# Three places instead of four for the gathered down rows, one query tile loaded ahead, and the first block's outputs joined

## The chip, the cores and the metric

The kernel runs on one core of one Trainium2 chip. Its time is the device time of one launch, in microseconds (us), as the median of three runs. The profile is of one more execution, taken by the hardware profiler.

## The reference, cut to what matters

256 tokens of 2048 channels go through a first block (retention, mLSTM, a mixture of experts called PEER) and a second block. All of it is float32. The change touches the outputs of the retention heads and the PEER layer:

```python
def step(s, inp):                       # retention, each of 8 heads
    att = jnp.einsum('bhcd,bhsd->bhcs', qc, kc) * intra
    y = jnp.einsum('bhcs,bhse->bhce', att, vc) + jnp.einsum('bhcd,bhde->bhce', qc * q_dec, s)
...
def block(tb):                          # PEER, each block of 128 tokens
    qh = (tb @ w_query).reshape(P_BLOCK, P_HEADS, 2, P_DQ // 2)
    s = jnp.einsum('thpd,hpkd->thpk', qh, sub_keys).astype(jnp.float32)
    sv, si = lax.top_k(s, P_TOPK)
    ...                                 # 16 of 16*16 pairs for each of 8 heads: eid [128, 8, 16]
    g = jax.nn.softmax(best_s, axis=-1)
    act = jax.nn.gelu(jnp.einsum('thkd,td->thk', expert_down[eid], tb).astype(jnp.float32), approximate=False)
    return jnp.einsum('thk,thkd->td', (g * act).astype(tb.dtype), expert_up[eid])
```

For each token 8 x 16 = 128 experts are picked, and for each pick one row of `expert_down` and one of `expert_up` is needed, 2048 numbers each.

## The kernel before, in words

The program is a row of phases on one core; each engine has its own instruction stream, written out in order, and waits on semaphores. The phases are an opening (to about 450 us), the first block (450 to 909 us), the PEER layer (909 to about 2265 us) and the second block (to the end).

**First block.** TensorE runs a dense projection: each "slot" m is 24 matmuls of 128x512 (L996, L997, L998). Small groups of other work are put between slots, by tables of slot numbers (L884 to L900): `TURN_AT`, `HEAD_AT`, `Y_AT` and so on. `scores(h)` (L1036) makes a pair's attention scores, `ret_out(h)` (L1048, L1050) the output of head h in PSUM bank V + h % 2, and ScalarE copies that output out in the same slot. `turn_y(f)` transposes the finished y in fills of four 128x128 pieces; ScalarE (`copy_hi`) and VectorE (`copy_lo`) split each fill into a high and a low part. ScalarE (L722) and GpSimd (L729) also make the high and low parts of the dense weights.

**PEER.** The query projection reads `peer_query` in tiles of 128x4x512, four tiles (slots 0 to 3) for each of four chunks of 512 columns. Chunk 0 is in the weight ring. The four tiles of chunk 1 are "early" tiles in other places that are free: `query_tile` (1,0), `key_scores` (1,1), `mem_kv` (1,2), `free_query_tile` (1,3). SyncE (L1707 to L1717) issues (1,3) at once, waits for `h2_ready`, issues the other three, and then loads chunks 2 and 3 into the ring, each when its slot is given free.

Tokens lie on the partitions, two blocks of 128, so 256 picks p, in 128 groups G of two. A row transfer (`indirect_dma_start`, GpSimd) fetches the row of pick p for 128 tokens at once: 128x2048 float32, 1.05 MB. D(p) is the down row, U(p) the up row. GpSimd's order in group G is D(2G), D(2G+1), U(2G), U(2G+1) (L1747 to L1775), each with its wait ahead of it:
- D(p) (L1758) has 4 places, `down_rows`, and waits for dot p-4, which frees the place. `down_rows` lies in the 32 KB per partition that the first block used for split weights.
- U(p) (L1766) has 4 places, `up_rows`, and waits for the adding of pick p-4: even picks are added by VectorE, odd ones by TensorE.

VectorE's order in group G is dot 2G, dot 2G+1 (L2272, each waits for its landing), a piece of the list work for later heads (L1575 to L1583, L2155 to L2207), and the adding of up row 2(G-1) (L2216 the first of a block, L2219). Between a dot and the adding stand ScalarE's gelu and share (L2047, L2053, L2059) and the diagonal (L2062) by which TensorE adds the odd row (L1909).

## Time and profile before

| | |
|---|---|
| median of 3 runs | 3403.07 us (3401.09 to 3404.42) |
| profiled execution | 3401.59 us, of it 3399.8 us span |
| TensorE busy, VectorE, GpSimd | 85%, 54%, 69% of the span |
| mean granted TensorE clock | 0.919 |
| row transfers (GpSimd's queue) | 536.90 MB, 37.5% of the 16 engines' span |

The busy shares are means over phases with different limits. What bounds a phase is read from the idle time of its engines and from what ended it: a row of the profile ends with the idle time in front of a group of instructions and its releaser. In the table of windows each engine has its busy time (and its count of instructions), then come the granted clock, the busy share of the 16 DMA engines (it can read slightly over 1), and GB/s.

### The profile page before, as it was taken

Reading aid. Unit: us, or ns where it says so; the run is one execution under the profiler, and the core shown is the slowest. Engines: PE = TensorE matmul, PEld = TensorE weight load, DVE = VectorE, ACT = ScalarE, POOL = GpSimd, SP = SyncE. Lnnn points to the kernel's source line nnn. Section 1 sums busy time; section 2 is a strip of 40 time slices with the busy share of each in tenths; the row PEclk is TensorE's granted clock in tenths of the full one; section 3 lists DMA queues with packets and bytes.
Section 4 is the critical chain, followed back from the end, with each engine's and each line's share of the span. In section 5 each row is a group of like instructions: output and inputs, shape, how many; then the busy total and the mean of one; then the engine's idle time right before and its main releaser. Section 6 shows DMA issues by size and latency. Waiting matters only on the chain. (4 is left out here: it accounts for less than half of the span.)

```text
span 3399.8 us, 30787 instructions
## 1 busy us (share of the span) xinstructions
PE 2904.0 (85%) x11248; PEld 2041.8 (60%) x11248; DVE 1824.3 (54%) x2377; ACT 1145.8 (34%) x1860; POOL 2338.9 (69%) x1120
## 2 busy tenths in 40 slices
PE   6999999999986666655656776589999999999998
PEld 2787888888753333322222322248888888888887
DVE  3577537412678777778988887751147412111122
ACT  3322456544421111111221112134455444444443
POOL 0244677588667575657776677868767698888887
PEclk8999999999988888877678887889999999999999
DMA  9999855365699999999999999985545456656554
GB/s 397 338 349 335 302 173 169 126 231 192 241 420 426 425 427 425 427 427 427 412 427 427 427 427 426 427 324 188 172 154 189 138 197 194 227 190 206 190 191 164
DMA packets 308075, 1015.86 MB, mean 299 GB/s; under 512 B 21932, under 2 KB 26640, under 8 KB 241104
## 3 DMA queue, kind: packets, MB, share of 16 engines
q1 hardware_dynamic: 231336, 475.62, 40.5%
q0 software_dynamic: 73728, 536.90, 37.5%
q8 instruction: 89, 1.46, 0.2%
q10 hardware_dynamic: 2860, 1.38, 0.1%
q14 instruction: 62, 0.51, 0.0%
HBM read 1009.59 MB, written 4.24 MB: 298 GB/s over the span
## 5 line engine op out<-in xcount | busy, mean ns | idle before, releaser
L729 POOL TENSOR_TENSOR block_weights_lo<-weight_ring,block_weights_hi 128x1024 fp32r<-128x1024 f32 x596 | 1444.3, 2432 | 577.7 <-ACT block_weights_hi L722 563.1
L1909 PE MATMUL banks<-up_rows,pick_diagonal 128*128 128x512 f32 x1024 | 681.3, 827 | 438.9 <-DMA up_rows<-peer_up,picked_experts 377.5
L722 ACT ACTIVATE block_weights_hi<-weight_ring 128x1024 fp32r<-128x1024 f32 x608 | 640.8, 1059 | 997.6 <-PE banks L3063 315.9
L1909 PEld LDWEIGHTS banks<-up_rows,pick_diagonal 128*128 128x128 f32 x1024 | 262.4, 269 | 826.4 <-issue 732.5
L1766 POOL DMA_INDIRECT up_rows<-peer_up,picked_experts x256 | 483.3, 1888 | 338.6 <-DVE expert_sum L2219 113.7
L2272 DVE CUSTOM_DVE_ANT_0 down_rows<-down_rows,h_tokens 128x2048 f32<-128x2048 f32 x256 | 583.7, 2291 | 184.1 <-DMA down_rows<-peer_down,picked_experts 179.4
L1758 POOL DMA_INDIRECT down_rows<-peer_down,picked_experts x256 | 405.4, 1584 | 101.3 <-issue 78.3
L2219 DVE SCALAR_TENSOR_TENSOR expert_sum<-up_rows,pick_share,expert_sum 128x2048 f32<-128x2048 f32 x125 | 293.9, 2352 | 51.4 <-ACT pick_share L2053 45.5
L2047 ACT ACTIVATE pick_gelu<-pick_dots 128x2 f32<-128x2 f32 x127 | 25.8, 203 | 834.0 <-DVE pick_dots L2272 833.7
L2497 PE MATMUL banks<-block_weights_hi,h_T_hi 128*128 128x512 f32 x688 | 272.8, 397 | 2.3 <-POOL block_weights_lo L729 2.3
L2499 PE MATMUL banks<-block_weights_hi,h_T_lo 128*128 128x512 f32 x688 | 268.3, 390 | 0.0
L2498 PE MATMUL banks<-block_weights_lo,h_T_hi 128*128 128x512 f32 x688 | 267.9, 389 | 0.0
L3061 PE MATMUL banks<-block_weights_hi,h_T_hi 128*128 128x512 f32 x640 | 250.2, 391 | 0.0
L3063 PE MATMUL banks<-block_weights_hi,h_T_lo 128*128 128x512 f32 x640 | 249.3, 390 | 0.0
L3062 PE MATMUL banks<-block_weights_lo,h_T_hi 128*128 128x512 f32 x640 | 249.1, 389 | 0.0
L602 DVE SCALAR_TENSOR_TENSOR banks<-cond_ring,cond_T,banks 128x512 f32<-128x512 f32 x224 | 169.3, 756 | 62.4 <-DMA cond_ring<-w_ada 55.4
L996 PE MATMUL banks<-block_weights_hi,h_T_hi 128*128 128x512 f32 x504 | 200.5, 398 | 1.9 <-PEq L218 1.0
L997 PE MATMUL banks<-block_weights_lo,h_T_hi 128*128 128x512 f32 x504 | 196.7, 390 | 0.0
L3127 DVE TENSOR_TENSOR gate<-banks,p_cols 128x512 f32<-128x512 f32 x32 | 20.6, 687 | 262.4 <-PE banks L3063 262.4
L998 PE MATMUL banks<-block_weights_hi,h_T_lo 128*128 128x512 f32 x384 | 149.7, 390 | 0.0
L2497 PEld LDWEIGHTS banks<-block_weights_hi,h_T_hi 128*128 128x128 f32 x688 | 129.3, 188 | 30.4 <-POOL block_weights_lo L729 4.5
L2499 PEld LDWEIGHTS banks<-block_weights_hi,h_T_lo 128*128 128x128 f32 x688 | 129.1, 188 | 27.4
(549 smaller groups left out, 4344.5 us busy)
## 6 DMA issues: line engine op xcount, KB each, us to landing
weight_ring<-w_in SPq DMA_DIRECT2D x232, 1024.0 KB, 4.9
cond_ring<-w_ada SPq DMA_DIRECT2D x128, 512.0 KB, 6.3
weight_ring<-w_ada SPq DMA_DIRECT2D x32, 1024.0 KB, 8.6
weight_ring<-w_out SPq DMA_DIRECT2D x32, 1024.0 KB, 4.9
weight_ring<-peer_query SPq DMA_DIRECT2D x12, 1024.0 KB, 17.1
weight_ring<-w_ret_out SPq DMA_DIRECT2D x8, 1024.0 KB, 4.9
weight_ring<-w_mlstm_out SPq DMA_DIRECT2D x8, 1024.0 KB, 4.9
weight_ring<-w_mem_kv SPq DMA_DIRECT2D x8, 1024.0 KB, 11.9
```

The costliest lines, as they stand in the source:

```text
L722: act.activation(self.hi[:, self.place(slot, h)], ring.tile[:, slot, h * self.HALF:(h + 1) * self.HALF], ACT.Copy).then_inc(self.hi_ready, 1)
L729: pool.tensor_tensor(self.lo[:, at], ring.tile[:, slot, h * self.HALF:(h + 1) * self.HALF], self.hi[:, at], ALU.subtract).then_inc(ring.us ...
L1758: pool.indirect_dma_start(down[:, p % ROWS], None, io["peer_down"][0], bass.IndirectOffsetOnAxis(ap=expert[:, p:p + 1], axis=0)).then_inc( ...
L1766: pool.indirect_dma_start(up[:, p % ROWS], None, io["peer_up"][0], bass.IndirectOffsetOnAxis(ap=expert[:, p:p + 1], axis=0)).then_inc(up_l ...
L1909: mm = pe.matmul(ps[:, 4 + b], diag[:, G % 2], up[:, p % ROWS, b * CG:(b + 1) * CG], start=(G % PER_TB == 0), stop=(G % PER_TB == PER_TB - ...
L2219: dve.scalar_tensor_tensor(acc[:], up[:, p % ROWS], share[:, p:p + 1], acc[:], ALU.mult, ALU.add).then_inc(even_added, 1)
L2272: dve.tensor_tensor_reduce(down[:, p % ROWS], down[:, p % ROWS], h2[:, G // PER_TB], 1.0, 0.0, ALU.mult, ALU.add, dots[:, p:p + 1]).then_i ...
L2497: pe.matmul(out, hi, w_hi, start=(k == 0), stop=False, skip_group_check=True)
L2498: pe.matmul(out, hi, w_lo, start=False, stop=False, skip_group_check=True)
L2499: mm = pe.matmul(out, lo, w_hi, start=False, stop=(k == KB - 1), skip_group_check=True)
L3061: pe.matmul(out, hi, w_hi, start=begin, stop=False, skip_group_check=True)
L3063: mm = pe.matmul(out, lo, w_hi, start=False, stop=end, skip_group_check=True)
```

## The change

Four edits.

1. Down rows have three places instead of four, so D(p) waits for dot p-3. The three landing semaphores and their counts follow.
2. The fourth place, 8 KB per partition, becomes `tiles_ahead`, which holds query tile (2,0). It is issued by SyncE right behind the early tiles; the ring loads only three tiles of chunk 2.
3. Each early tile waits for what frees its own place: (1,3) for nothing, (1,1) until the first block's products are done (`e.split.free`), (1,0) for the second `x1_ready`, (1,2) for `h2_ready`. The order is (1,3), (1,1), (1,0), (1,2), (2,0).
4. In the first block the output of an even head is made one slot later, together with that of its odd partner (`OUT_AT`), and the eight y fills come as four in every second slot instead of two in each (`y_fill_at`).

```diff
@@ -884,6 +884,7 @@
         HEAD_AT = [STATE_AT + 3 + h for h in range(R_HEADS)]
+        OUT_AT = [HEAD_AT[h // 2 * 2 + 1] + 1 for h in range(R_HEADS)]
         LF_AT, SUM_AT = HEAD_AT[2], HEAD_AT[-1] + 1
@@ -892,6 +893,7 @@
         Y_AT = M_GATED + 1
+        y_fill_at = lambda f: Y_AT + f // 4 * 2
         columns_at = lambda g: SLOTS * (g + 1) + (3 if g == 0 else 0)
@@ -1136,7 +1138,7 @@
                 for h in range(R_HEADS):
-                    if m == HEAD_AT[h] + 1:
+                    if m == OUT_AT[h]:
                         ret_out(h)
@@ -1157,7 +1159,7 @@
                 for f in range(FILLS):
-                    if m == Y_AT + f // 2:
+                    if m == y_fill_at(f):
                         turn_y(f)
@@ -1232,7 +1234,7 @@
                 for h in range(R_HEADS):
-                    if m == HEAD_AT[h] + 1:
+                    if m == OUT_AT[h]:
                         act.wait_ge(y_done, h + 1)
@@ -1269,7 +1271,7 @@
                 for f in range(FILLS):
-                    if m == Y_AT + f // 2:
+                    if m == y_fill_at(f):
                         copy_hi(f, y_turned, lambda k: y_hi[:, k], y_hi_out)
@@ -1527,7 +1529,7 @@
                 for f in range(FILLS):
-                    if m == Y_AT + f // 2:
+                    if m == y_fill_at(f):
                         copy_lo(f, y_hi_out, lambda k: y_hi[:, k], lambda k: y_lo[:, k], y_lo_out)
@@ -1597,7 +1599,7 @@
         base, N, NB = ring.turn, HP * PEER_K // CG, CG // P
-        GROUPS, ROWS = TB * PICKS // 2, 4
+        GROUPS, ROWS, DOWN_ROWS = TB * PICKS // 2, 4, 3
         next_turn = base + N + 2 * MEM_W // CG
@@ -1620,7 +1622,7 @@
             return 8 * r - 6 if r < PEER_H else 8 * PEER_H - 6 + 6 * (r - PEER_H)
-        down, up = nc.alloc_sbuf_tensor_at("down_rows", [P, ROWS, D], F32, offset=e.split2_at), sb("up_rows", [P, ROWS, D])
+        down, up = nc.alloc_sbuf_tensor_at("down_rows", [P, DOWN_ROWS, D], F32, offset=e.split2_at), sb("up_rows", [P, ROWS, D])
         scores, acc = sb("key_scores", [P, HP, TB, PEER_K]), sb("expert_sum", [P, D])
@@ -1646,8 +1648,12 @@
                                     free_tile[:])
+        SPARE_ROWS = ROWS - DOWN_ROWS
+        ahead = nc.alloc_sbuf_tensor_at("tiles_ahead", [P, SPARE_ROWS, TILE_K, CG], F32, offset=e.split2_at + DOWN_ROWS * D * 4)
+        early_tile = {(EARLY_CHUNK, s): tile for s, tile in enumerate(early_query)}
+        early_tile.update({(EARLY_CHUNK + 1, s): ahead[:, s] for s in range(SPARE_ROWS)})
         gt2_row, GATE_ROW = spare_tile[0:1].rearrange("p a n -> p (a n)"), PER_TB - 8
-        query_tile = lambda n, s: early_query[s] if n == EARLY_CHUNK and s < len(early_query) else ring.tile[:, s]
+        query_tile = lambda n, s: early_tile[n, s] if (n, s) in early_tile else ring.tile[:, s]
 
@@ -1666,13 +1672,13 @@
         h2_ready, turned, turned_out = sem("h2_ready"), sem("h2_turned"), sem("h2_turned_out")
-        early_query_in = [sem(f"early_query_in{s}") for s in range(len(early_query))]
+        early_query_in = {(n, s): sem(f"early_query_in{n}_{s}") for n, s in early_tile}
         gt2_row_in, gt2_row_spread = sem("gt2_row_in"), sem("gt2_row_spread")
...
         picks_ready, weights_ready, go = sem("picks_ready"), sem("weights_ready"), sem("gather_go")
-        down_landed = [sem(f"down_landed{s}") for s in range(ROWS)]
+        down_landed = [sem(f"down_landed{s}") for s in range(DOWN_ROWS)]
         up_landed = [sem(f"up_landed{s}") for s in range(ROWS)]
@@ -1702,17 +1708,22 @@
         in_turn = lambda p: 16 * (p // ROWS + 1)
+        down_in_turn = lambda p: 16 * (p // DOWN_ROWS + 1)
         block = ctx.enter_context(phase_block(nc, e))
...
         def _(sp):
-            for s, tile in sorted(enumerate(early_query), reverse=True):
-                if s == len(early_query) - 2:
+            for n, s in [(EARLY_CHUNK, s) for s in (3, 1, 0, 2)] + [(EARLY_CHUNK + 1, s) for s in range(SPARE_ROWS)]:
+                if (n, s) == (EARLY_CHUNK, 1):
+                    sp.wait_ge(e.split.free, e.split.free_after(e.split_tiles))
+                if (n, s) == (EARLY_CHUNK, 0):
+                    sp.wait_ge(x1_ready, TB)
+                if (n, s) == (EARLY_CHUNK, 2):
                     sp.wait_ge(h2_ready, TB * H_FILLS)
-                sp.dma_start(tile, k_tile(io["peer_query"][0], s, slice(EARLY_CHUNK * CG, (EARLY_CHUNK + 1) * CG))).then_inc(early_query_in[s], 16)
+                sp.dma_start(early_tile[n, s], k_tile(io["peer_query"][0], s, slice(n * CG, (n + 1) * CG))).then_inc(early_query_in[n, s], 16)
             for n in range(1, N):
                 load_tiles(sp, ring, turn_of(io["peer_query"][0], slice(n * CG, (n + 1) * CG)), base + n,
-                           skip=len(early_query) if n == EARLY_CHUNK else 0)
+                           skip=sum(1 for of, _ in early_tile if of == n))
             sp.dma_start(gt2_row, e.mod_rows[0, 3 * D:4 * D].unsqueeze(0)).then_inc(gt2_row_in, 16)
@@ -1752,11 +1763,11 @@
                 for p in (2 * G, 2 * G + 1):
-                    if p >= ROWS:
-                        pool.wait_ge(dot_done, p - ROWS + 1)
+                    if p >= DOWN_ROWS:
+                        pool.wait_ge(dot_done, p - DOWN_ROWS + 1)
                         pool.sem_inc(go, 1)
-                    pool.indirect_dma_start(down[:, p % ROWS], None, io["peer_down"][0],
-                                            bass.IndirectOffsetOnAxis(ap=expert[:, p:p + 1], axis=0)).then_inc(down_landed[p % ROWS], 16)
+                    pool.indirect_dma_start(down[:, p % DOWN_ROWS], None, io["peer_down"][0],
+                                            bass.IndirectOffsetOnAxis(ap=expert[:, p:p + 1], axis=0)).then_inc(down_landed[p % DOWN_ROWS], 16)
                 if G == 0:
@@ -1781,8 +1792,8 @@
                         pe.wait_ge(q_out, u - 1)
-                    if nb == 0 and n == EARLY_CHUNK and s < len(early_query):
-                        pe.wait_ge(early_query_in[s], 16)
+                    if nb == 0 and (n, s) in early_tile:
+                        pe.wait_ge(early_query_in[n, s], 16)
                         pe.sem_inc(ring.landed[s], 16)
@@ -2268,8 +2279,8 @@
                 for p in (2 * G, 2 * G + 1):
-                    dve.wait_ge(down_landed[p % ROWS], in_turn(p))
-                    dve.tensor_tensor_reduce(down[:, p % ROWS], down[:, p % ROWS], h2[:, G // PER_TB], 1.0, 0.0, ALU.mult, ALU.add,
+                    dve.wait_ge(down_landed[p % DOWN_ROWS], down_in_turn(p))
+                    dve.tensor_tensor_reduce(down[:, p % DOWN_ROWS], down[:, p % DOWN_ROWS], h2[:, G // PER_TB], 1.0, 0.0, ALU.mult, ALU.add,
                                              dots[:, p:p + 1]).then_inc(dot_done, 1)
```

GpSimd's stream at the start of the gather, before and then after. In brackets stand the semaphores by the names of their first use in the program: `cond_summed` is here the count of dots, `cond_stored` that of even rows added, `h1_out` that of odd rows added. "x2" is two instructions of the same form.

```order
L1758 DMA down_rows<-peer_down,picked_experts 128x2048 [waits ctx_turned]
L1758 DMA down_rows<-peer_down,picked_experts 128x2048
L1766 DMA up_rows<-peer_up,picked_experts 128x2048 [waits rows_turned]
L1766 DMA up_rows<-peer_up,picked_experts 128x2048
L1758 DMA down_rows<-peer_down,picked_experts 128x2048 x2
L1766 DMA up_rows<-peer_up,picked_experts 128x2048 x2
L1758 DMA down_rows<-peer_down,picked_experts 128x2048 [waits cond_summed] x2
L1766 DMA up_rows<-peer_up,picked_experts 128x2048 [waits cond_stored]
L1766 DMA up_rows<-peer_up,picked_experts 128x2048 [waits h1_out]
```

```order
L1769 DMA down_rows<-peer_down,picked_experts 128x2048 [waits ctx_turned_out]
L1769 DMA down_rows<-peer_down,picked_experts 128x2048
L1777 DMA up_rows<-peer_up,picked_experts 128x2048 [waits rows_turned]
L1777 DMA up_rows<-peer_up,picked_experts 128x2048
L1769 DMA down_rows<-peer_down,picked_experts 128x2048
L1769 DMA down_rows<-peer_down,picked_experts 128x2048 [waits cond_summed]
L1777 DMA up_rows<-peer_up,picked_experts 128x2048 x2
L1769 DMA down_rows<-peer_down,picked_experts 128x2048 [waits cond_summed] x2
L1777 DMA up_rows<-peer_up,picked_experts 128x2048 [waits cond_stored]
L1777 DMA up_rows<-peer_up,picked_experts 128x2048 [waits h1_out]
```

No row changes its place; the wait for a dot begins one row earlier, at D(3), and each later down row waits for one dot more.

SyncE's stream at the start of PEER, before and then after; `silu_done` is here the count of `h2_ready`, `gates_done` that of `x1_ready`, and `block1_weights_free` is the freeing of the first block's products.

```order
L1712 DMA free_query_tile<-peer_query 128x4x512
L1712 DMA mem_kv<-peer_query 128x4x512 [waits silu_done]
L1712 DMA key_scores<-peer_query 128x4x512
L1712 DMA query_tile<-peer_query 128x4x512
L180 DMA weight_ring<-peer_query 128x4x512 [waits weight_used] x8
```

```order
L1723 DMA free_query_tile<-peer_query 128x4x512
L1723 DMA key_scores<-peer_query 128x4x512 [waits block1_weights_free]
L1723 DMA query_tile<-peer_query 128x4x512 [waits gates_done]
L1723 DMA mem_kv<-peer_query 128x4x512 [waits silu_done]
L1723 DMA tiles_ahead<-peer_query 128x4x512
L180 DMA weight_ring<-peer_query 128x4x512 [waits weight_used] x7
```

Two tiles come out from behind the wait for `h2_ready`, one tile more is issued behind it, and the ring loads one less.

TensorE's stream in the first block where the output of head 1 stands: before, and then after. The output of head 0 stood 24 dense matmuls earlier.

```order
L998 MATMUL banks<-block_weights_hi,h_T_lo 128x512
L1048 MATMUL banks<-lat_cols,mixer_space 128x128 [waits att_ready]
L1048 MATMUL banks<-lat_cols,mixer_space 128x128
L1050 MATMUL banks<-mixer_space 128x128
L1048 MATMUL banks<-lat_cols,mixer_space 128x128 x2
L1050 MATMUL banks<-mixer_space 128x128
L1036 MATMUL banks<-mixer_space 128x256 [waits att_ready]
L1036 MATMUL banks<-mixer_space 128x256 x3
L996 MATMUL banks<-block_weights_hi,h_T_hi 128x512 [waits block1_weights_first_ready]
```

```order
L1000 MATMUL banks<-block_weights_hi,h_T_lo 128x512
L1050 MATMUL banks<-lat_cols,mixer_space 128x128 [waits att_ready]
L1050 MATMUL banks<-lat_cols,mixer_space 128x128
L1052 MATMUL banks<-mixer_space 128x128
L1050 MATMUL banks<-lat_cols,mixer_space 128x128 x2
L1052 MATMUL banks<-mixer_space 128x128
L1050 MATMUL banks<-lat_cols,mixer_space 128x128 [waits att_ready]
L1050 MATMUL banks<-lat_cols,mixer_space 128x128
L1052 MATMUL banks<-mixer_space 128x128
L1050 MATMUL banks<-lat_cols,mixer_space 128x128 x2
L1052 MATMUL banks<-mixer_space 128x128
L1038 MATMUL banks<-mixer_space 128x256 [waits att_ready]
```

The six matmuls of head 0 moved here from the slot before; the scores behind them and the dense stream are as they were.

## Rows read from the trace of the kernel before

**Rows 1.** Timeline of TensorE, 505 to 510 us (start, duration, instruction).
```profile
505.33 0.39 PE L998 MATMUL banks<-block_weights_hi,h_T_lo 128*128 128x512 f32 x1
505.86 0.71 PE L1048 MATMUL banks<-lat_cols,mixer_space 128*128 128x128 f32 x4
...
508.46 0.50 PE L996 MATMUL banks<-block_weights_hi,h_T_hi 128*128 128x512 f32 x1
508.80 0.39 PE L997 MATMUL banks<-block_weights_lo,h_T_hi 128*128 128x512 f32 x1
509.03 0.39 PE L998 MATMUL banks<-block_weights_hi,h_T_lo 128*128 128x512 f32 x1
```

**Rows 2.** The page's groups: busy, mean ns, idle before, its releaser.
```profile
L2272 DVE CUSTOM_DVE_ANT_0 down_rows<-down_rows,h_tokens 128x2048 f32<-128x2048 f32 x256 | 583.7, 2291 | 184.1 <-DMA down_rows<-peer_down,picked_experts 179.4
```

**Rows 3.** Windows: us, PE, PEld, DVE, ACT, POOL busy, PEclk, DMA share, GB/s.
```profile
920.00:925.00 5.00, 5.00 (x48) 5.00 (x47) 3.29 (x10) 0.28 (x1) 0.00 (x0) 1.00 0.33 89
...
1200.00:1600.00 400.00, 257.83 (x547) 122.66 (x545) 313.77 (x398) 63.37 (x186) 258.39 (x154) 0.80 1.01 426
...
1620.00:1660.00 40.00, 24.07 (x32) 9.42 (x32) 39.06 (x57) 9.01 (x21) 27.31 (x17) 0.66 1.00 402
1660.00:1700.00 40.00, 22.99 (x35) 8.64 (x33) 34.88 (x51) 8.26 (x21) 33.84 (x18) 0.74 1.01 420
```

**Rows 4.** Timeline of SyncE's queue, 905 to 1330 us.
```profile
922.11 0.37 SPq L1712 DMA_DIRECT2D mem_kv<-peer_query  x1
...
1093.96 200.38 SPq L180 DMA_DIRECT2D weight_ring<-peer_query  x8
```

**Rows 5.** Timeline of GpSimd and VectorE, 928 to 986 us.
```profile
930.30 1.11 POOL L1758 DMA_INDIRECT down_rows<-peer_down,picked_experts  x1 [22.99 <-DVE picked_experts L2186]
...
944.57 0.94 POOL L1758 DMA_INDIRECT down_rows<-peer_down,picked_experts  x1 [0.30 <-issue]
952.93 2.20 POOL L1766 DMA_INDIRECT up_rows<-peer_up,picked_experts  x1 [7.43 <-DVE expert_sum L2216]
...
968.89 0.94 POOL L1758 DMA_INDIRECT down_rows<-peer_down,picked_experts  x1 [0.30 <-issue]
...
952.04 2.29 DVE L2272 CUSTOM_DVE_ANT_0 down_rows<-down_rows,h_tokens 128x2048 f32<-128x2048 f32 x1
...
954.25 2.29 DVE L2272 CUSTOM_DVE_ANT_0 down_rows<-down_rows,h_tokens 128x2048 f32<-128x2048 f32 x1
...
975.16 2.29 DVE L2272 CUSTOM_DVE_ANT_0 down_rows<-down_rows,h_tokens 128x2048 f32<-128x2048 f32 x1
```

**Rows 6.** Tile down_rows: landing of the issues at 930.30, 944.57, 968.89, 1645.33.
```profile
DMA to landing us min/median/max: 5.8/5.8/5.8
DMA to landing us min/median/max: 15.8/15.8/15.8
DMA to landing us min/median/max: 11.1/11.1/11.1
DMA to landing us min/median/max: 11.7/11.7/11.7
```

**Rows 7.** Timeline of GpSimd and VectorE, 1614 to 1662 us.
```profile
1645.33 1.07 POOL L1758 DMA_INDIRECT down_rows<-peer_down,picked_experts  x1 [0.30 <-issue]
...
1651.33 2.29 DVE L2272 CUSTOM_DVE_ANT_0 down_rows<-down_rows,h_tokens 128x2048 f32<-128x2048 f32 x1
```

**Rows 8.** The same, 2196 to 2232 us.
```profile
2209.86 0.94 POOL L1758 DMA_INDIRECT down_rows<-peer_down,picked_experts  x1 [0.31 <-issue]
...
2213.34 2.29 DVE L2272 CUSTOM_DVE_ANT_0 down_rows<-down_rows,h_tokens 128x2048 f32<-128x2048 f32 x1 [0.18 <-DMA down_rows<-peer_down,picked_experts]
...
2223.12 2.29 DVE L2272 CUSTOM_DVE_ANT_0 down_rows<-down_rows,h_tokens 128x2048 f32<-128x2048 f32 x1 [0.15 <-DMA down_rows<-peer_down,picked_experts]
```

**Rows 9.** Timeline of VectorE, 1674 to 1690 us.
```profile
1684.05 2.29 DVE L2272 CUSTOM_DVE_ANT_0 down_rows<-down_rows,h_tokens 128x2048 f32<-128x2048 f32 x1 [0.74 <-DMA down_rows<-peer_down,picked_experts]
...
1687.46 2.32 DVE L2272 CUSTOM_DVE_ANT_0 down_rows<-down_rows,h_tokens 128x2048 f32<-128x2048 f32 x1 [1.11 <-DMA down_rows<-peer_down,picked_experts]
```

## The prediction

> **What bounds the kernel now.** I read the page's lines by engine first, then the windows of the gather, then the timelines of GpSimd, VectorE and SyncE. The change touches two stages with different limits.
>
> In the first block TensorE runs one dense matmul every 0.23 us (508.80 to 509.03), and what counts is what is put between them [rows 1]. A dense matmul starts at 505.33, so the next could at 505.56; the inserted output of a head starts at 505.86, after a wait of 0.30 us. The first dense matmul after an inserted group comes 0.34 us before its follower (508.46 to 508.80), 0.11 more than usual.
>
> The gather is bound by the DMA. VectorE's dot products, 256 of 2.29 us, lie idle 184.1 us before them, and 179.4 of that ends with the landing of a down row [rows 2]. From 1200 to 1600 us the DMA engines are busy 1.01 of the time and move 426 GB/s [rows 3], so a row of 1.05 MB takes 1.05 / 0.426 = 2.46 us, and a group G of two down and two up rows 9.8. Two stretches are different: at the start of the gather and around G 64 to 70 (1614 to 1662 us) the dots do not wait for landings, VectorE is behind. From 1620 to 1660 it is busy 39.06 of 40 us and the DMA moves only 402 GB/s [rows 3]. Everything else in the gather is cover. So two questions decide: how many bytes lie in the saturated stretch, and whether GpSimd still issues rows early enough.
>
> **The first block.** Four pairs of heads' outputs are joined, and four groups of y transposes become two of twice the size in every second slot: six fewer places where a group interrupts the dense stream. The matmuls inserted stay the same. At most this saves 6 x 0.11 = 0.66 us, plus the 0.30 us wait (the even output comes a slot later) [rows 1], 0.96 in all; at least nothing. On the other side a joined pair fills both banks at once, and its copies on ScalarE come together one slot later; ScalarE must also write weights for the dense stream. Nothing in the trace of before shows that bunching; I allow 0.5 us of loss. I take -0.5, range -1.0 to +0.5.
>
> **The tiles.** SyncE issues the four query tiles of chunk 1 without, or with earlier, waits, where before three of them wait until 922.11 [rows 4]. From 920 to 925 us the DMA is busy only 0.33 of the time [rows 3], so they cost nothing there and one more tile fits: (2,0). It used to be one of eight ring loads issued from 1093.96 on [rows 4], in the saturated stretch. One tile is 128x4x512 f32, 1.05 MB, as large as a row: 2.46 us leave the saturated stretch. The other three (1,x) tiles were outside it already. Do earlier tiles start the gather earlier? The first down row is issued at 930.30 after a wait for picked_experts, a chain that needs none of these tiles [rows 5]. So -2.45, and nothing for the start.
>
> **Three places for down rows.** A down row p now waits for dot p-3 instead of p-4. For an even row nothing changes that matters: dot 2G-3 closes the previous group's pair. The odd row 2G+1 waited for dot 2G-3 and now waits for the first dot of the group before, 2G-2, and everything queued behind it on GpSimd (two up rows, the next down row) moves with it. Two prices of GpSimd come from rows. A waiting issue starts 0.8 us after its releaser. And an issue that begins while a wide VectorE operation runs ends 0.8 us after that operation: the issue at 952.93 takes 2.20 us and ends at 955.13, the dot that ran ended at 952.04 + 2.29 = 954.33 [rows 5]. So where two dots run back to back, the odd row's issue, released by the first, ends 0.8 after the second. The last price is from an issue's end to landing with an empty line: the first row is issued at 930.30 in 1.11 us and lands 5.8 after its start [rows 5, 6], 5.8 - 1.11 = 4.7 us.
>
> The start, where before's dots are back to back and late:
> - D5 was issued at 944.57 and landed 15.8 later, at 960.4 [rows 5, 6]. Now it waits for dot 2, dot 3 runs from 954.25 to 956.54, the issue ends at 957.34, landing 962.0 at the earliest: 1.7 late.
> - D9 was issued at 968.89 and landed at 980.0. Now dot 7 (975.16 to 977.45) holds it until 978.25, landing 982.95: 3.0 late. D7 by the same steps lies between.
> VectorE's own times do not move meanwhile, since it is behind; so the shift at the end of the stretch is the largest excess: +3.0.
>
> Around G 64 to 70 the same: D139 was issued at 1645.33 and landed 11.7 later, 1657.03. Dot 137 (1651.33 to 1653.62) now holds it to 1654.42, landing 1659.1: 2.1 late [rows 6, 7]; the others of the stretch are less late. +2.1.
>
> By the Trainium skill, "SBUF — State Buffer", section "SBUF: two separate sides", a GpSimd descriptor write locked out by a VectorE operation goes on about 115 ns after that operation. The trace shows 0.8 us to the end of the issue [rows 5], so the measurement decides; with 0.1 in its place both excesses would be 0.7 smaller, 3.7 us in all instead of 5.1.
>
> Elsewhere VectorE waits for landings. Take G 124 and 125. D251 was issued at 2209.86 and done at 2210.80. Now it is released by dot 248, which ends 0.18 us before dot 249 begins, and so starts near 2214.0 with dot 249 running (2213.34 to 2215.63) and ends at 2216.43; + 4.7 = 2221.1, while it is due at 2223.12 [rows 8]. 2.0 us of slack: no hole. But its lead before landing falls from 12.3 to 6.7 us. What a line that thin costs is bounded as follows. Below: nothing, by that slack. Above: after the late stretch the line of before is thin too, and there the DMA moved 420 GB/s instead of 426 in 40 us [rows 3], 0.6 us lost in four groups, seen as two landings 3.41 us apart (1684.05, 1687.46) instead of 2.46 [rows 9]. 0.14 us for each of some 110 groups is 15. That stretch starts thin from a state with a full line, so I do not carry the rate through; the nearest row is that of the slack. I take +3, a fifth of the upper end.
>
> **Sum.** Against the profiled execution's 3401.59: -0.5 - 2.45 + 3.0 + 2.1 + 3 = +5.15, 3406.7. The median of the runs, 3403.07, is 1.48 above that execution, so I expect 3408.2, written 3408. About 0.2%, 6.8 us, is what a measurement of this kernel can tell from no change; the forecast lies inside it.
>
> **Rivals.**
> - A, the places are free. D5's hole is filled by rows whose landing was only bookkeeping, because the 16 DMA engines run apart and the line's bytes do not go missing; the thin line costs nothing. Then -0.5 - 2.45 and at most 1 of the 5.1: 3399.6, against the median 3401. For it: VectorE is behind in both stretches, so a row that lands late need not make its dot late. Against it: the DMA dips to 402 GB/s in just such a stretch [rows 3]: bytes not moved there are not made up. Chance 0.27.
> - B, the thin line costs in each group. Place: the issue of the odd down row, released by the group's first dot and held by the second, in all groups of the steady stretch; its price decides once it is above 0.04 us a group (4.6 us in all), for then the sum passes 6.8. With 0.10 us in 110 groups: -2.95 + 5.1 + 11 = +13, 3416. At 0.14 3421. For it: rows 9 show a landing late while its issue was done in time. Against it: 2.0 us of slack. Chance 0.28.
> - C, no effect of places or tile that can be told, all terms cancel: 3403 within 2. Chance 0.10, inside the bound.
> The forecast, 3404 to 3411, has 0.35.
>
> **From the cases.** Faster by over 0.2% would need more than all gains together (3.4 us) and stays at 0.04. Slower by over 0.2% (above 3409.9) takes B and what of the forecast's case could spill over its own range: 0.35. Within: 0.61. The range goes from 3399.5 (A, with the run's own spread of 1.7) to 3419 (B near its upper price); the forecast's own range is 3404 to 3411.
>
> **What will show it.** Right: D5 lands 1.7 and D9 3.0 us later against the gather's first issue, the shift near G 60 is about +0.5, the rows after G 71 another 2 later; SyncE issues seven ring loads instead of eight for the query; the dense stream has no 0.30 us wait at the second output; down issues in the steady stretch end 0.8 us after the second dot. Wrong: GB/s in 1200 to 1600 below 424 (then B); the odd rows' issues ending before the second dot; a gather shorter than before by 2 us or more (A); a first block that moves by more than 1 us either way.

## The result, and the profile after

| | before | after |
|---|---|---|
| median of 6 runs each | 3402.32 us | 3423.44 us |
| after over before, 95% interval | | 1.0064, 1.0052 to 1.0075 |
| span of the profiled execution | 3399.8 us | 3422.0 us |

One of the six runs after, 4585.89 us at a mean granted clock of 0.583 where the others had 0.92, is a slow one; the ratio leaves it out, and the median of the other five is 3423.10 us.

The change makes the kernel 21 us slower, 0.6%. The forecast of 3408 and its range to 3419 were too low; rival B, at its upper price (3421), is what happened.

The page of the changed kernel shows it in the groups that answer to [rows 2] (busy us, mean ns, idle us before and what ended it), and so does what GpSimd waited for (us, times, longest).

```profile
L1769 POOL DMA_INDIRECT down_rows<-peer_down,picked_experts x256 | 505.7, 1975 | 367.4 <-DVE pick_dots L2283 290.5
L2283 DVE CUSTOM_DVE_ANT_0 down_rows<-down_rows,h_tokens 128x2048 f32<-128x2048 f32 x256 | 584.3, 2291 | 210.1 <-DMA down_rows<-peer_down,picked_experts 206.4
```

```profile
POOL down_rows L1769 <- DVE pick_dots L2283: 290.5, 78, 7.6
POOL up_rows L1777 <- issue: 78.0, 256, 0.3
```

GpSimd, which issues all rows, now idles 290.5 us for dots in front of down rows, at 78 of them; before no down row waited for a dot. The up rows behind them never wait for a place of their own. In the kernel before they did:

```profile
POOL up_rows L1766 <- DVE expert_sum L2219: 113.7, 36, 5.0
POOL up_rows L1766 <- PE banks L1909: 100.3, 39, 5.6
```

With two smaller entries (41.9 and 14.1 us) that was 270 us, so GpSimd does not wait much longer than before. What has changed is where it waits: ahead of the odd down row, with both up rows queued behind it. All rows are issued closer to their landing. In the packet records of 1170 to 2230 us the median row packet starts 7.7 us after the end of its row's issue before the change, and 5.1 us after it. VectorE in turn waits 206.4 us for landings (before 179.4).

The windows that answer to [rows 3], changed kernel:

```profile
920.00:925.00 5.00, 4.63 (x41) 4.44 (x41) 2.54 (x10) 0.56 (x2) 0.00 (x0) 1.00 1.02 369
1200.00:1600.00 400.00, 254.45 (x546) 122.60 (x545) 311.11 (x395) 62.29 (x182) 261.24 (x151) 0.80 1.01 419
1620.00:1660.00 40.00, 24.59 (x32) 9.51 (x32) 38.60 (x52) 7.93 (x17) 21.01 (x14) 0.68 0.98 388
1700.00:2200.00 500.00, 326.41 (x589) 132.04 (x588) 401.03 (x487) 96.08 (x252) 357.98 (x196) 0.81 1.01 419
```

The tiles fill the hole at 920 (0.33 busy before, 1.02 now). But the steady stretch moves 419 GB/s instead of 426, with the DMA engines still shown as busy, and the stretch around 1640 falls from 402 to 388.

To place the loss I followed single dots, by counting them in VectorE's timeline. These are dots 18, 28, 46, 129, 142 and 255, of the kernel before:

```profile
1028.01 2.29 DVE L2272 CUSTOM_DVE_ANT_0 down_rows<-down_rows,h_tokens 128x2048 f32<-128x2048 f32 x1 [1.61 <-DMA down_rows<-peer_down,picked_experts]
1078.18 2.29 DVE L2272 CUSTOM_DVE_ANT_0 down_rows<-down_rows,h_tokens 128x2048 f32<-128x2048 f32 x1
1176.71 2.28 DVE L2272 CUSTOM_DVE_ANT_0 down_rows<-down_rows,h_tokens 128x2048 f32<-128x2048 f32 x1
1607.76 2.29 DVE L2272 CUSTOM_DVE_ANT_0 down_rows<-down_rows,h_tokens 128x2048 f32<-128x2048 f32 x1 [1.40 <-DMA down_rows<-peer_down,picked_experts]
1674.24 2.29 DVE L2272 CUSTOM_DVE_ANT_0 down_rows<-down_rows,h_tokens 128x2048 f32<-128x2048 f32 x1 [0.96 <-DMA down_rows<-peer_down,picked_experts]
2242.74 2.29 DVE L2272 CUSTOM_DVE_ANT_0 down_rows<-down_rows,h_tokens 128x2048 f32<-128x2048 f32 x1 [0.15 <-DMA down_rows<-peer_down,picked_experts]
```

and the same dots of the changed kernel:

```profile
1031.92 2.29 DVE L2283 CUSTOM_DVE_ANT_0 down_rows<-down_rows,h_tokens 128x2048 f32<-128x2048 f32 x1 [2.45 <-DMA down_rows<-peer_down,picked_experts]
1082.74 2.28 DVE L2283 CUSTOM_DVE_ANT_0 down_rows<-down_rows,h_tokens 128x2048 f32<-128x2048 f32 x1
1177.89 2.29 DVE L2283 CUSTOM_DVE_ANT_0 down_rows<-down_rows,h_tokens 128x2048 f32<-128x2048 f32 x1 [0.58 <-DMA down_rows<-peer_down,picked_experts]
1615.82 2.29 DVE L2283 CUSTOM_DVE_ANT_0 down_rows<-down_rows,h_tokens 128x2048 f32<-128x2048 f32 x1 [1.37 <-DMA down_rows<-peer_down,picked_experts]
1687.74 2.29 DVE L2283 CUSTOM_DVE_ANT_0 down_rows<-down_rows,h_tokens 128x2048 f32<-128x2048 f32 x1 [0.93 <-DMA down_rows<-peer_down,picked_experts]
2264.83 2.29 DVE L2283 CUSTOM_DVE_ANT_0 down_rows<-down_rows,h_tokens 128x2048 f32<-128x2048 f32 x1 [0.15 <-DMA down_rows<-peer_down,picked_experts]
```

The first row is issued at 928.82 instead of 930.30, so the ledger starts at -1.5 (how little of that is the first block's edit stands under e1_first_block):

| stretch | shift at its end | change | forecast |
|---|---|---|---|
| until the first issue | -1.5 | -1.5 | -0.5 |
| dots 0 to 18 (VectorE behind) | +3.9 | +5.4 | +3.0 |
| 18 to 28 | +4.6 | +0.7 | |
| 28 to 46 (chunk 2's tiles) | +1.2 | -3.4 | -2.45 |
| 46 to 129 (42 groups) | +8.1 | +6.9 | |
| 129 to 142 (VectorE behind) | +13.5 | +5.4 | +2.1 |
| 142 to 255 (57 groups) | +22.1 | +8.6 | |

The three stretches without an entry under forecast sum to 16.2 us. There the forecast had 3. The ledger compares one execution with one, and single stretches differ by some us from one execution to another: from dot 46 to 129 and from 142 to 255 together the changed kernel loses 15.5 us, and two kernels of the experiments with the same later wait (e3 and e9) 10.1 us each.

### The profile page after: what moved, and what is told of

Same layout as the page of the kernel before. It is cut to its first block and busy times, and to the rows that moved or that the text cites. A ratio compares the mean times of both kernels' runs of the same rounds, so it can differ in the third digit from the quotient of the medians.

```text
span 3422.0 us, 30787 instructions
## 1 busy us (share of the span) xinstructions
PE 2895.2 (85%) x11248; PEld 2039.2 (60%) x11248; DVE 1824.3 (53%) x2377; ACT 1145.8 (33%) x1860; POOL 2361.3 (69%) x1120
## 3 DMA queue, kind: packets, MB, share of 16 engines
q0 software_dynamic: 73728, 536.90, 37.9%
## 5 line engine op out<-in xcount | busy, mean ns | idle before, releaser
L1920 PE MATMUL banks<-up_rows,pick_diagonal 128*128 128x512 f32 x1024 | 673.5, 819 | 466.7 <-DMA up_rows<-peer_up,picked_experts 421.5
L1769 POOL DMA_INDIRECT down_rows<-peer_down,picked_experts x256 | 505.7, 1975 | 367.4 <-DVE pick_dots L2283 290.5
L2283 DVE CUSTOM_DVE_ANT_0 down_rows<-down_rows,h_tokens 128x2048 f32<-128x2048 f32 x256 | 584.3, 2291 | 210.1 <-DMA down_rows<-peer_down,picked_experts 206.4
L1777 POOL DMA_INDIRECT up_rows<-peer_up,picked_experts x256 | 404.6, 1580 | 78.0 <-issue 78.0
## 6 DMA issues: line engine op xcount, KB each, us to landing
weight_ring<-peer_query SPq DMA_DIRECT2D x11, 1024.0 KB, 15.5
```

The costliest lines, as they stand in the source:

```text
L1769: pool.indirect_dma_start(down[:, p % DOWN_ROWS], None, io["peer_down"][0], bass.IndirectOffsetOnAxis(ap=expert[:, p:p + 1], axis=0)).then ...
L1777: pool.indirect_dma_start(up[:, p % ROWS], None, io["peer_up"][0], bass.IndirectOffsetOnAxis(ap=expert[:, p:p + 1], axis=0)).then_inc(up_l ...
L1920: mm = pe.matmul(ps[:, 4 + b], diag[:, G % 2], up[:, p % ROWS, b * CG:(b + 1) * CG], start=(G % PER_TB == 0), stop=(G % PER_TB == PER_TB - ...
L2283: dve.tensor_tensor_reduce(down[:, p % DOWN_ROWS], down[:, p % DOWN_ROWS], h2[:, G // PER_TB], 1.0, 0.0, ALU.mult, ALU.add, dots[:, p:p + ...
```

## The experiments

Each median stands beside that of the kernel before on the same chip: 3401.36 (e1 to e4), 3401.91 (e6 to e9), 3401.66 (e10 to e12), 3400.93 (e13). The diffs are cut to the lines that matter.

**e1_first_block: the first block alone.** From the kernel before:

```diff
+        OUT_AT = [HEAD_AT[h // 2 * 2 + 1] + 1 for h in range(R_HEADS)]
-                    if m == HEAD_AT[h] + 1:
+                    if m == OUT_AT[h]:
+        y_fill_at = lambda f: Y_AT + f // 4 * 2
-                    if m == Y_AT + f // 2:
+                    if m == y_fill_at(f):
```

> Only the first block's edit: outputs of two heads joined, four y fills in every second slot; the gather as before. In the changed kernel the gather's first row was issued at 928.82 instead of 930.30. Theory: 1.5 us come from the first block's dense stream (six interruptions less, one wait of 0.3 us less), so here the first row is issued near 928.8 and the time is 1 to 2 us under before, about 3401. Rival: the 1.5 us come from the tiles' own waits; then this run is the same as before within 0.5 us and its first row is issued at 930.2 to 930.4.

Measured 3400.73, ratio 0.9999 (0.9990 to 1.0008). The first row is issued at 929.78, 0.5 us earlier than before:

```profile
929.78 1.11 POOL L1763 DMA_INDIRECT down_rows<-peer_down,picked_experts  x1 [23.14 <-DVE picked_experts L2191]
```

Neither expectation fits. The -1.5 of the changed kernel comes in two parts. The first is there before any edited instruction has run. The last dense matmul ahead of the first inserted group starts 0.9 us earlier (first row: kernel before, second: changed kernel):

```profile
453.49 0.39 PE L998 MATMUL banks<-block_weights_hi,h_T_lo 128*128 128x512 f32 x1
452.62 0.39 PE L1000 MATMUL banks<-block_weights_hi,h_T_lo 128*128 128x512 f32 x1
```

The second is the stretch from there to the first row's issue, 476.8 us before and 476.2 after. Over all 14 traces this stretch has two values, some 0.6 us apart, with the edit and without: 476.8 four times and 476.3 once (e3) without it, 476.7 five times and 476.1 to 476.2 four times with it. Between like values the edit gains 0.1 us. The time of e1 can't tell that from 0 or from 0.5.

**e2_tile_waits: the tiles' order and waits alone.** `SPARE_ROWS` is 0 here, so there is no tile ahead.

```diff
-            for s, tile in sorted(enumerate(early_query), reverse=True):
-                if s == len(early_query) - 2:
+            for n, s in [(EARLY_CHUNK, s) for s in (3, 1, 0, 2)] + [(EARLY_CHUNK + 1, s) for s in range(SPARE_ROWS)]:
+                if (n, s) == (EARLY_CHUNK, 1):
+                    sp.wait_ge(e.split.free, e.split.free_after(e.split_tiles))
+                if (n, s) == (EARLY_CHUNK, 0):
+                    sp.wait_ge(x1_ready, TB)
+                if (n, s) == (EARLY_CHUNK, 2):
                     sp.wait_ge(h2_ready, TB * H_FILLS)
```

> Only the early tiles' order and own waits; four places for down rows, no tile ahead, first block as before. Theory: the tiles land before TensorE asks for them either way, so the first row's issue stays at 930.3 and the time within 1 us of before, 3402. Rival: tiles that no longer share the DMA with the first rows start the gather earlier: first row issued or landed 1 us or more earlier, time 1 to 2 us under before.

Measured 3400.65, ratio 0.9998 (0.9989 to 1.0007). First issue 930.41:

```profile
916.35 0.37 SPq L1721 DMA_DIRECT2D key_scores<-peer_query  x1
917.80 0.37 SPq L1721 DMA_DIRECT2D query_tile<-peer_query  x1
922.22 0.37 SPq L1721 DMA_DIRECT2D mem_kv<-peer_query  x1
```

```profile
930.41 1.11 POOL L1767 DMA_INDIRECT down_rows<-peer_down,picked_experts  x1 [23.00 <-DVE picked_experts L2195]
```

As expected by the theory: `key_scores` and `query_tile` leave 6.2 and 5.3 us earlier (922.52 and 923.07 before), and nothing follows.

**e3_three_places: three places alone.**

```diff
-        GROUPS, ROWS = TB * PICKS // 2, 4
+        GROUPS, ROWS, DOWN_ROWS = TB * PICKS // 2, 4, 3
-                    if p >= ROWS:
-                        pool.wait_ge(dot_done, p - ROWS + 1)
+                    if p >= DOWN_ROWS:
+                        pool.wait_ge(dot_done, p - DOWN_ROWS + 1)
```

> Only three places for down rows (the fourth place stays empty, no tile ahead, all four ring tiles of chunk 2 loaded in the gather, tile waits and first block as before). Theory (the thin line costs all along: 16 DMA engines, each with hiccups of its own, can't run apart when little is queued, so their hiccups add up): the whole loss is here, +24 to +28 us over before (the measured +21 plus what the tile and the first block gave, 2.5 and 1.5), with 419 GB/s in 1200 to 1600 us and the landings of a row spread over 1 to 3 us instead of 3 to 6. Rival (late issues only: holes where VectorE is behind, nothing elsewhere): +5 us and 426 GB/s in 1200 to 1600. Rival (the tile ahead or the new tile waits disturb the gather): +5 to +10, the rest in other runs.

Measured 3423.11, ratio 1.0062 (1.0048 to 1.0075), 22 us over its before. 419 GB/s in 1200 to 1600, 422 in 1700 to 2200. The whole loss is here, a little less than expected, because the tile ahead shows no gain in the changed kernel's time. "Late issues only" falls. The expectation on the landings came true: the completion of a row is told in 16 increments of its semaphore, and from the first to the last of them it is 3.9 us before and 1.6 us here (medians, 1170 to 2230 us). That fits the theory's picture of DMA engines that can no longer run apart; that this is what costs is not shown by it.

**e4_all_but_places: the first block and the tile waits, four places.** The change without `DOWN_ROWS` and `tiles_ahead`.

> Four places for down rows and no tile ahead, but the first block's edit and the tiles' own waits. Theory: the sum of the two parts that cost nothing, 1 to 2 us under before, about 3401, with 426 GB/s in 1200 to 1600. Rival (the parts disturb the gather): over 3403 with a lower GB/s in the gather.

Measured 3401.24, ratio 0.9999 (0.9990 to 1.0009), 426 GB/s in 1200 to 1600. The harmless parts together give nothing that can be told from no change.

**e9_four_places_waits_of_three: the place or the wait?**

```diff
-                    if p >= ROWS:
-                        pool.wait_ge(dot_done, p - ROWS + 1)
+                    if p >= 3:
+                        pool.wait_ge(dot_done, p - 3 + 1)
```

> The kernel before with four places for down rows, each row however waiting for the dot that the three-place kernel waits for (dot p-3). Theory (the moment of issue is all; which place a row lands in is nothing): as three places alone, 3420 to 3426, 419 GB/s. Rival (with three places the rows' addresses or the semaphores' turn cost something): 3402 to 3415.

Measured 3426.84, ratio 1.0077 (1.0061 to 1.0092). Four places with the later wait lose as much as three places do. The moment of issue is the cause; the place gives no loss that can be told.

**e12_waits_of_three_late: the later wait in the steady stretch only.** The condition is `p - (3 if G >= 72 else ROWS) + 1`.

> The kernel before (four places), with the three-place kernel's waits (dot p-3) only in groups 72 to 127, where VectorE is never behind. Theory (the thin line costs in every group, because packets that are moved soon after their issue take longer): 56 groups at 0.14 us, +8 us (6 to 11), 3408 to 3413, with 419 to 423 GB/s in 1700 to 2200 and 426 in 1200 to 1600. Rival (the loss comes from late issues in the stretches where VectorE is behind, G 1 to 9 and 64 to 70, and what follows from them): 0 to +2 us, 426 GB/s in both windows.

Measured 3409.08, ratio 1.0020 (1.0011 to 1.0029): +7.4 us over its before, where the theory said 8 and the rival 0 to 2. Its windows:

```profile
1200.00:1600.00 400.00, 253.42 (x543) 120.79 (x542) 314.51 (x396) 62.45 (x184) 263.94 (x155) 0.80 1.01 426
1700.00:2200.00 500.00, 327.12 (x589) 133.57 (x590) 397.21 (x471) 95.23 (x249) 365.97 (x195) 0.81 1.01 418
```

426 GB/s without the later wait and 418 with it, in one execution. The loss is not even: of these 500 us the part from 1950 to 2050 alone falls to 403 GB/s, where the changed kernel has 422. 0.14 us a group is a mean of bursts.

**e6_odd_down_last: another order on GpSimd.** If the odd row's wait is the trouble, put it behind the two up rows:

```diff
-                for p in (2 * G, 2 * G + 1):            # D, D, then U, U
+                for down_row, p in rows_of(G):          # D(2G), U(2G), U(2G+1), D(2G+1)
```

> The changed kernel with one more edit: in each group but the first and the last, GpSimd issues the odd down row behind the two up rows (down, up, up, down). Three places, one tile ahead. The odd row still waits for the first dot of the group before, but it is due two rows (4.9 us) later and no up row is queued behind that wait. Theory (what costs is the thin line that the odd row's wait leaves, not the number of places): issues are again 9 us or more ahead of their landing, 426 GB/s in 1200 to 1600, and the time is before's less what the tile ahead takes out of the saturated stretch (2.5) and the first block gives: 3397 to 3400. Rival (three places are too few, whatever the order): 3415 to 3424 and 419 to 422 GB/s. Rival (the odd row lands last, so the adding comes 4.9 us later and the up rows' places come free too late): a new wait at the up rows, over 3410.

Measured 3510.46, ratio 1.0322 (1.0304 to 1.0340). The theory's number failed by 110 us, and the third expectation is right. What GpSimd waited for:

```profile
POOL up_rows L1780 <- DVE expert_sum L2233: 162.5, 46, 5.3
POOL up_rows L1780 <- PE banks L1923: 128.8, 68, 5.0
POOL down_rows L1774 <- DVE pick_dots L2286: 112.8, 35, 6.6
```

The odd row lands last, its dot is late, and so are the adding of both up rows and their places. The up rows wait for places again, 291 us, and the down rows still wait 113 us for dots: 404 us together, where the changed kernel has 290. 397 GB/s in 1200 to 1600.

**e7_odd_down_last_four** is that order with four places and no tile ahead.

> The order down, up, up, down with four places, no tile ahead, first block's edit and tile waits as in the changed kernel. Theory: the line was thick enough with four places, so this order gives nothing in the steady stretch (426 to 427 GB/s) and up to 3 us where VectorE is behind: 3398 to 3402. Rival (more lead is worth more without end): 3395 or less, with over 428 GB/s.

Measured 3520.96, ratio 1.0334 (1.0319 to 1.0349). Its down rows have no wait for a dot, and GpSimd waits over 400 us in front of up rows (246.7 for VectorE's adding, 150.6 for TensorE's). A fourth down place doesn't help here; the order costs.

**e8_odd_down_last_two** has that order with two down places and two tiles ahead.

> The order down, up, up, down with only two places for down rows and two query tiles ahead. The odd row 2G+1 now waits for dot 2G-1, which ends about 7.4 us before it is due; the lead of its issue is then 5.5 to 6.5 us, as thin as in the changed kernel (6.7). Theory: a loss of the same kind and size as there or somewhat more, 414 to 420 GB/s in 1200 to 1600, 3418 to 3435. Rival (only the number of rows in flight counts: seven in the changed kernel, six here): clearly more than there, over 3440. Rival (only the odd row's place in the order counts): near e6_odd_down_last.

Measured 3685.47, ratio 1.0835 (1.0818 to 1.0851): far over the theory's range and over 3440, as the second expectation said, and not near e6. Lead counted for a new order was not to be trusted. GpSimd waited 725.7 us for dots, at 181 down rows, and the DMA stood at 361 GB/s in 1200 to 1600.

**e10_odd_up_first** and **e11_down_up_down_up** ask whether the order's loss is a matter of which rows are neighbours.

```diff
-  ((1, 0), (0, 0), (0, 1), (1, 1))      # e7: D(2G), U(2G), U(2G+1), D(2G+1)
+  ((1, 0), (0, 1), (0, 0), (1, 1))      # e10: D(2G), U(2G+1), U(2G), D(2G+1)
+  ((1, 0), (0, 0), (1, 1), (0, 1))      # e11: D(2G), U(2G), D(2G+1), U(2G+1)
```

> As e7_odd_down_last_four (four places), but in each group the order down 2G, up 2G+1, up 2G, down 2G+1: the odd down row is still last, yet no two neighbours in the line are the down and the up row of the same pick. e7_odd_down_last_four took 3521. Theory (the adding comes 4.9 us later because the second dot does; the up rows' places come free later and the line gets thin): the same loss again, 3500 to 3535. Rival (a down and an up row of the same pick, at the same place of two tables, disturb each other when they are moved side by side): back to 3400 to 3415.

> As e7_odd_down_last_four, but down 2G, up 2G, down 2G+1, up 2G+1: the odd down row is one row later than in the kernel before instead of two, and both pairs of neighbours are of the same pick. Theory (lateness): the dot comes 2.45 instead of 4.9 us later, so a part of the loss of e7_odd_down_last_four, 3415 to 3470. Rival (same pick side by side): the full loss or more, 3520 or over.

Measured 3604.46 (1.0597, 1.0581 to 1.0614) and 3423.65 (1.0071, 1.0055 to 1.0086). e7 and e11 have the same pairs side by side and lose 119 and 22 us, and e10, without any, loses most: the rival is out. (e10 also issues the odd up row ahead of the even one, so it is no test of the neighbours alone.) In e10 the wait in front is the odd up row's, for TensorE's adding, which comes last of all:

```profile
POOL up_rows L1778 <- PE banks L1921: 570.9, 105, 12.5
```

The size of e10 was outside my range too; lateness was the right direction, and its price is larger than I said.

**e13_tile_left_out: what a tile is worth.** Four places; TensorE reads tile (1,3) where it should read (2,0), which is not loaded, so this part of the computation is not the reference's.

> Four places for down rows, the first block's edit and the tiles' own waits, and query tile (2,0) is not loaded at all: TensorE reads the early tile (1,3) in its stead, so the queries of chunk 2 are not the reference's. It asks what the tile ahead was worth at most. Theory: 1.05 MB less in the saturated stretch, seven ring loads instead of eight: 2.45 us under e4_all_but_places (3401.2), about 3399. Rival: the tile's bytes are hidden, 3401 (the changed kernel and three places alone were 3423.4 and 3423.1, with no gain to be seen).

Measured 3400.23, ratio 0.9996 (0.9987 to 1.0005): 0.7 us under its before, with an interval from 4.4 under to 1.7 over. This does not tell 2.45 from 0. Against the trace of before its dots gain 2.1 us between dots 32 and 40, where chunk 2's tiles travel; at the last dot 0.7 us of gain on the first issue is left. What a tile is worth in the end stays open; 0 and 2.45 us both fit.

## Where the thin line's time goes

The DMA engines are shown as busy all along, and still move less. The row queue's line of the DMA view for 1700 to 2200 us (packets, MB, their time as a share of 16 engines) before,

```profile
q0 software_dynamic: 28563, 208.00, 98.5%
```

and with the changed kernel:

```profile
q0 software_dynamic: 28045, 204.22, 98.2%
```

A mean packet takes 0.985 x 16 x 500 / 28563 = 0.2759 us before and 0.982 x 16 x 500 / 28045 = 0.2801 us after, 1.5% longer, where the throughput falls by 1.9% (427 to 419). So most of the loss is not an empty line: it is packets that take longer. (The mean is below the 0.309 us of a row packet because it takes in small packets of 4 bytes, one for every eight row packets.) Over the whole run the page's line points the same way:

```profile
q0 software_dynamic: 73728, 536.90, 37.9%
```

37.9% of 3422.0 is 1297 us, against 1275 us before (37.5% of 3399.8), for the same bytes. Shares with one decimal leave 3 us to either side of that difference. Added up packet by packet from the records of the traces it is 1295.4 against 1275.7 us: 19.7 of the 23.6 us by which the gather got longer (from -1.5 to +22.1 in the ledger).

Nearly all row packets of 8 KB take 0.309 us in every kernel; the loss is a tail above 0.36 us. In e3_three_places, from 1170 to 2230 us, that tail is 47% of the packets that are moved 1.0 to 1.6 us after the end of their row's issue, 15% at 1.6 to 2, 6% at 2 to 2.5, 1.8% at 3 to 4 and 0.5% at 6 to 8.

In the kernel before under 1% of the row packets are moved within 3 us of their issue, in e3 7%. So these early packets are few, and they are not the whole tail. In the changed kernel the row packets of this stretch take 14.3 us more than before (their time divided by 16 engines). Of that, 7.1 us fall on packets moved 4 to 6 us after their issue: 2.1% of those are long, against 0.7% at the same distance before. That the later issue causes the loss is shown by e9 and e12, which change nothing else. Why packets then take longer was not tested; that they are moved soon after their issue goes with it and does not explain all of it.

One row as an example, D249 in the changed kernel: GpSimd's issue, and then VectorE's dots 248 and 249, each of which starts with its row's landing.

```profile
2223.91 2.42 POOL L1769 DMA_INDIRECT down_rows<-peer_down,picked_experts  x1 [2.29 <-DVE pick_dots L2283]
```

```profile
2230.62 2.29 DVE L2283 CUSTOM_DVE_ANT_0 down_rows<-down_rows,h_tokens 128x2048 f32<-128x2048 f32 x1 [2.14 <-DMA down_rows<-peer_down,picked_experts]
2234.61 2.29 DVE L2283 CUSTOM_DVE_ANT_0 down_rows<-down_rows,h_tokens 128x2048 f32<-128x2048 f32 x1 [1.69 <-DMA down_rows<-peer_down,picked_experts]
```

The issue ended at 2226.33, 4.3 us before the row ahead of it landed (2230.62); by the 4.7 us of an empty line it could have landed at 2231.0 and was due at 2233.1. It landed at 2234.6. This is the 2.0 us of slack of the prediction, there in full (2.1), and 1.5 us lost all the same.

## Why the prediction was wrong, step by step

- **First block, -0.5: too large, and of no weight.** Between traces of like value the edit gives 0.1 us. The six places where a group interrupts the dense stream are gone, as forecast. But a joined group takes 4.06 us from dense matmul to dense matmul (488.24 to 492.30), where its two parts had 1.48 and 2.72, less one dense step of 0.23: 3.97. And the wait was not saved. Between the outputs of the heads 2 and 3 a group starts 0.55 us after the one ahead of it where 0.22 is usual, 0.33 late against 0.30 before:

```profile
504.43 0.39 PE L1052 MATMUL banks<-mixer_space 128*128 128x128 f32 x2
504.98 0.71 PE L1050 MATMUL banks<-lat_cols,mixer_space 128*128 128x128 f32 x4 [0.16 <-DVE mixer_space L1331]
```

- **Tiles' own waits, 0: right** (e2).
- **Tile ahead, -2.45: not refuted.** The ledger shows -3.4 over dots 28 to 46, where e3, without the tile, has +1.5; by the end nothing is left of it (3423.4 with the tile, 3423.1 without). e13 can't size it.
- **The wait of the odd row and its hold by the second dot: right in mechanism.** D5 was forecast to be issued until 957.34, or 955.9 with the gather 1.5 us earlier; it ended at 956.18, and D9, forecast for 978.25, or 976.8, at 977.09:

```profile
953.97 2.21 POOL L1769 DMA_INDIRECT down_rows<-peer_down,picked_experts  x1 [7.45 <-DVE pick_dots L2283]
974.88 2.21 POOL L1769 DMA_INDIRECT down_rows<-peer_down,picked_experts  x1 [4.97 <-DVE pick_dots L2283]
```

```profile
984.07 2.29 DVE L2283 CUSTOM_DVE_ANT_0 down_rows<-down_rows,h_tokens 128x2048 f32<-128x2048 f32 x1 [1.27 <-DMA down_rows<-peer_down,picked_experts]
```

- **Its price where VectorE is behind, 3.0 + 2.1: too small by half, and the sum had the wrong rows.** It was 5.4 + 5.4. Two steps failed. First, D9's dot starts with its landing at 984.07, 7.0 us after the issue ended, where I had allowed 4.7. The 4.7 us of the very first row is the price with nothing else in the line, and I used it for a row behind others that are late as well. (For D5, behind an empty line, it held: landed 4.5 us after the end of its issue.) Second, I took the lateness of a row's landing for the shift of its dot. VectorE was behind, so before the change D9 lay landed for 3.9 us until its dot began:

```profile
983.90 2.28 DVE L2272 CUSTOM_DVE_ANT_0 down_rows<-down_rows,h_tokens 128x2048 f32<-128x2048 f32 x1
```

  Against the gather's first issue D9 landed 5.6 us later (forecast 3.0), but its dot moved only 1.7. The other 3.7 us of the 5.4 came at dots 14 to 18, which the forecast did not follow. In the second stretch it is the same: the shift grows at dots 138 and 140, by 2.2 and 2.6 us, and only by 0.3 at dot 139, the one that was priced.
- **The thin line, +3 of 0 to 15: the step that failed.** It was 16.2 by the ledger. The 0.14 us a group that I worked out of the windows after the late stretch and then set aside ("I do not carry the rate through") was right in kind and size: (6.9 + 8.6) / 99 groups = 0.16 in the changed kernel, 10.1 / 99 = 0.10 in e3 and e9, and e12 gives 7.4 / 56 = 0.13. That it came out so near is partly luck: it rests on 420 GB/s in 40 us, and in the other traces with the early wait (e1, e2, e4, e13) the same window (1660 to 1700 us) has 413 to 425. The reason given for the small value was the 2.0 us of slack. Slack in time of issue says that the line will not be empty. It does not say that a short line moves as fast as a long one.
- **Rows 9 showed it in the kernel before.** The row that landed at 1687.46 there was issued until 1679.79, 4.3 us before the row ahead of it landed (1684.05), just as D249 now:

```profile
1677.65 2.14 POOL L1758 DMA_INDIRECT down_rows<-peer_down,picked_experts  x1 [0.30 <-issue]
```

- **Rival A**, free places, is refuted by e3; **rival C** by the result. Rival B had the place, the kind and the price, at 0.28, under a forecast that had 0.35. Its own upper price gave 3421, above the 3419 at which the range ended.
- **The Trainium skill's 115 ns** ("SBUF — State Buffer", section "SBUF: two separate sides"), for a GpSimd descriptor write behind a VectorE operation: the changed kernel's held issues again end about 0.8 us after it (D249: dot at 2223.23 + 2.29 = 2225.52, issue done at 2226.33). The measurement stands.

## What to carry to other kernels

In a gather that saturates the DMA, don't price a later issue by whether the queue runs empty. Look for a stretch of the same trace in which the queue is already short, take the GB/s there against the GB/s elsewhere, in more than one execution, and multiply it by the whole length; a small difference, 1.5%, was 10 to 16 us here. And when a row is moved within a cycle, follow each row's dot and adding round to the place that they free: three orders that issue the odd down row later, with all four places, cost 22, 119 and 203 us.

## What I had not expected of the hardware

With rows issued closer to their landing, 1.8% of the row packets of 1170 to 2230 us took over 0.36 us (0.25% before) where nearly all others take 0.309, and the DMA engines were shown as busy (1.01) at 419 GB/s as at 426. One row less on its way, 1.05 MB, cost 21 us of 1320.
